# Seven block products for the last 22 gate tiles, and a new start, in a hybrid encoder layer on one core

## What is computed

```python
u = x @ w_in[l]                                # 1024 x 1024 times 1024 x 7688
ua, ub, uc, ug = _split(u, GROUP_COLS)         # gated DeltaNet, RWKV-7, window attention, gates
oa = _gdn_branch(ua, ...)                      # chunks of 64 tokens: inverse of (I + lower) per chunk and head
ob, v_first = _rwkv7_branch(ub, ...)
oc = _swa_branch(uc, swa_sinks[l])
gates = jax.nn.sigmoid(ug).reshape(bsz, t, N_BRANCH, d)        # 3072 columns: 24 tiles of 128
merged = gates[:, :, 0] * (oa @ w_branch_a[l]) + ...
```

## Time and profile before

| What | Value |
|---|---|
| median of three executions | 1816.58 us |
| span of the profiled execution | 1816.2 us (0.4 us under the median) |
| TensorE matmuls busy | 1781.5 us, 98% of the span |
| VectorE, ScalarE, GpSimd busy | 63%, 37%, 32% |
| DMA | 293 MB, 161 GB/s on average |
| stage one | 0 to 749 us, of it the last 22 tiles from about 508 us |
| stage two (scan) | 749.6 to about 922 us |
| stage three | the rest |

### The profile page before, as it was taken

One profiled execution on the slowest core, in us unless ns is written; L12 is line 12 of the kernel. 1 busy time (PEld: TensorE's weight loads), 2 busy tenths in 40 slices (PEclk: granted clock), 3 DMA queues, 4 the chain that ended last, 5 costly groups with the idle time before them and its releaser, 6 DMA issues. The chain is left out here.

```text
span 1816.2 us, 28096 instructions
## 1 busy us (share of the span) xinstructions
PE 1781.5 (98%) x11148; PEld 1471.3 (81%) x11148; DVE 1141.4 (63%) x1354; ACT 665.2 (37%) x1126; POOL 584.6 (32%) x418
## 2 busy tenths in 40 slices
PE   8999999999999999999999999999999999999997
PEld 7778787777788888788878788888888888888886
DVE  2856665666419930377768854966666665665577
ACT  3534434244421211355542231343333333344341
POOL 1211222212213332344415452755455554500000
PEclk9999999999999999999999999999999999999999
DMA  6255575235673377377665573225545455488464
GB/s 178 50 112 140 141 180 138 65 76 155 166 206 93 93 162 228 126 237 245 186 211 173 163 236 97 101 70 183 171 133 171 143 175 179 139 286 300 169 226 155
DMA packets 386434, 293.24 MB, mean 161 GB/s; under 512 B 172428, under 2 KB 318412, under 8 KB 384256
## 3 DMA queue, kind: packets, MB, share of 16 engines
q1 hardware_dynamic: 310080, 237.63, 44.1%
q10 hardware_dynamic: 76224, 53.81, 10.3%
HBM read 196.33 MB, written 94.98 MB: 160 GB/s over the span
## 5 line engine op out<-in xcount | busy, mean ns | idle before, releaser
L168 PE MATMUL bank<-xhi,w_hi 128*128 128x512 f32 x960 | 379.0, 395 | 2.5 <-ACT turned L847 1.7
L170 PE MATMUL bank<-xhi,w_lo 128*128 128x512 f32 x960 | 374.4, 390 | 0.0
L169 PE MATMUL bank<-xlo,w_hi 128*128 128x512 f32 x960 | 373.8, 389 | 0.0
L472 POOL TENSOR_TENSOR w_lo<-w_raw,w_hi 128x1024 fp32r<-128x1024 f32 x59 | 168.3, 2853 | 538.1 <-ACT w_hi L854 538.1
L168 PEld LDWEIGHTS bank<-xhi,w_hi 128*128 128x128 f32 x960 | 180.3, 188 | 43.3 <-issue 6.8
L170 PEld LDWEIGHTS bank<-xhi,w_lo 128*128 128x128 f32 x960 | 180.2, 188 | 38.4
L169 PEld LDWEIGHTS bank<-xlo,w_hi 128*128 128x128 f32 x960 | 180.4, 188 | 36.1
L2044 POOL TENSOR_TENSOR ff_ring_lo<-ff_w_sums,ff_ring_hi 128x512 fp32r<-128x512 f32 x88 | 125.7, 1430 | 74.6 <-ACT ff_ring_hi L2326 74.4
L2044 POOL TENSOR_TENSOR ff_ring_lo<-ff_raw,ff_ring_hi 128x512 fp32r<-128x512 f32 x66 | 96.2, 1460 | 149.4 <-ACT ff_ring_hi L2326 149.4
L834 ACT ACTIVATE work<-bank 128x512 f32<-128x512 f32 x68 | 40.7, 598 | 244.7 <-PE bank L170 228.4
L175 PE MATMUL b_ps<-x1hi,ff_ring_hi 128*128 128x512 f32 x264 | 102.9, 390 | 0.0
(11 more groups left out here) (418 smaller groups left out, 3968.7 us busy)
## 6 DMA issues: line engine op xcount, KB each, us to landing
w_raw<-in_w_in ACTq DMA_DIRECT2D x61, 512.0 KB, 4.3
hid_ops<-y SPq DMA_DIRECT2D x77, 256.0 KB, 2.8
ff_raw<-hid_ops SPq DMA_DIRECT2D x77, 256.0 KB, 3.9
op<-opnd SPq DMA_DIRECT2D x16, 1152.0 KB, 5.5
u<-work ACTq DMA_DIRECT2D x68, 256.0 KB, 4.3
b_gate<-u SPq DMA_DIRECT2D x24, 512.0 KB, 3.6
ff_raw<-in_ffn_gate SPq DMA_DIRECT2D x22, 512.0 KB, 4.5
ff_raw<-in_ffn_up SPq DMA_DIRECT2D x22, 512.0 KB, 5.7
```

What stands on the lines that cost most here:

```text
L168: pe.matmul(out, w_hi, x_hi, start=first, stop=False)
L169: pe.matmul(out, w_hi, x_lo, start=False, stop=False)
L170: return pe.matmul(out, w_lo, x_hi, start=False, stop=last)
L472: pool.tensor_tensor(w_lo[b][:, :, :], w_raw[b][:, :, :], as_f32(w_hi[b][:, :, :]), ALU.subtract).then_inc(w_lo_done, 1)
```

## The change

1. The last 22 gate tiles are taken as 11 pairs. Three blocks of x (512 inner by 512 tokens) and four sums of blocks, made once, are multiplied with blocks and sums of blocks of the pair's weights: seven products of 12 matmuls a pair (`product`), 77 in all, in the order of `seven_products(11)`. ScalarE makes the high part of each product's weights and GpSimd the low part, in a ring of four; VectorE makes four weight sums a pair and adds products to results held in SBUF (`settle`); ScalarE moves first parts out of PSUM (`snap`), applies the sigmoid (`close`) and stores.
2. The inversion is issued in between: in each slot j of VectorE's loop over the 77 products, from slot 12 on, as many of its instructions as fit a written-out room of 2.5 us less 0.7 us for each other instruction. `settle(j)` waits for the end of product j.
3. Ahead of the block's end only chunk 0 is loaded and waited for. Chunk 1 is issued after product (7, 10) without waiting for it; chunk 2 is loaded in the scan, after the first quarter of the attention's operands and the signal for chunk 1.
4. Start: 28 idle matmuls of 128 columns run on TensorE ahead of the first turn; the first weight load is issued after the first tile of x has landed, not at once.
5. The tile of the attention's values is moved forward in the order, with its own buffer, and its two turns come after RWKV's. The last two turns of head 3 follow products 0 and 1.
6. The gpsimd DMA scratch is cut to 512 (no transfer is issued there), and tiles are laid out anew.

```diff
+IDLE_PRODUCTS = 28
...
-    fillers = [*range(U_SQ, U_SV), *range(U_Z, A_TILES), U_SV, *range(U_GATE, U_GATE + 24)]
+    fillers = [U_SQ, U_SV, *range(U_SQ + 1, U_SV), *range(U_Z, A_TILES), *range(U_GATE, U_GATE + 24)]
...
+NR, NPAIRS = 39, 11
...
+    PAIRS = [(ORDER[NR + 2 * f], ORDER[NR + 2 * f + 1]) for f in range(NPAIRS)]
+    ORDER = ORDER[:NR]
...
-        turn_after[max(at + 1, 2 * at_tile[U_SV] + 2) + g] = ("value", g)
+        turn_after[max(q for q in turn_after if turn_after[q][0] == "rwkv") + 1 + g] = ("value", g)
...
+    LATE = [turn_after[q] for q in sorted(turn_after) if q >= NQ]
...
         def _(pool):
+            pool.memset(work[:, 17, 0:P], 0.0).then_inc(early_zeroed, 1)
...
+            def low_part(i):
+                p, f = SEQ[i]
+                src = pair_raw[f % 2][:, raw_block[p], :] if p in raw_block else part_sum[p]
+                pool.wait_ge(w_hi_done, NT_IN + i + 1)
+                pool.tensor_tensor(lo_pair[:, slot_of(i), :], src, as_f32(hi_pair[:, slot_of(i), :]), ALU.subtract).then_inc(w_lo_done, 1)
...
-            for c in range(DEEP):
-                load_chunk(sp, c, early, opnd, xinv, early_landed, early_inv)
-                sp.wait_ge(early_landed, 112 * c + 112)
-                sp.wait_ge(early_inv, 48 * c + 48)
+            load_chunk(sp, 0, early, opnd, xinv, early_landed, early_inv)
+            sp.wait_ge(early_landed, 112)
+            sp.wait_ge(early_inv, 48)
             sp.wait_ge(cols_landed, 16 * 17)
+            sp.wait_ge(mm_p, AT[7, NPAIRS - 1] + 1)
+            load_chunk(sp, 1, early, opnd, xinv, early_landed, early_inv)
...
+            pe.wait_ge(early_zeroed, 1)
+            for _ in range(IDLE_PRODUCTS):
+                pe.matmul(bank[3][:, 0:P], work[:, 17, 0:P], work[:, 17, 0:P], start=True, stop=True)
             pe.wait_ge(const_landed, 16)
...
+            def product(i):
+                p, f = SEQ[i]
+                pe.wait_ge(w_lo_done, NT_IN + i + 1)
...
+                for k in range(4):
+                    cols_ = slice(k * P, (k + 1) * P)
+                    last = more_dot(pe, to, hi_pair[:, slot_of(i), cols_], lo_pair[:, slot_of(i), cols_], hi[:, k, :], lo[:, k, :], p in (1, 2, 7) and k == 0)
+                last.then_inc(mm_p, 1)
+            for i in range(len(SEQ)):
+                product(i)
+                if i < len(LATE):
+                    turn_tokens(LATE[i])
...
+            act.wait_ge(x_landed[0], 16)
             load_w(0)
             split(0)
             load_w(1)
...
+            def high_part(i):
...
+                if i < RING:
+                    act.wait_ge(mm_done, done_at[NQ - 3 if i < 2 else NQ - 1])
+                else:
+                    act.wait_ge(mm_p, i - RING + 1)
...
+            def settle(j):
+                p, f = SEQ[j]
+                to, before, src = {2: (11, 1, z_bank), 5: (22, 5, y_bank(f)), 4: (21, 6, y_bank(f))}[p]
+                dve.wait_ge(mm_p, j + 1)
+                dve.wait_ge(snapped, SNAP_AT[before, f])
+                dve.tensor_tensor(result_of(to, f), result_of(to, f), src, ALU.add).then_inc(added, 1)
...
+                        yield 0.07 + (PARTS[k].stop - PARTS[k].start) * i * i * (0.0019 if done % 2 else 0.00115)
+            inversion, room = invert(), 0.0
+            for j in range(len(SEQ)):
+                p, f = SEQ[j]
+                work_now = 0
+                if p in (2, 5, 4) and j < len(SEQ) - 1:
+                    settle(j)
+                    work_now += 1
...
+                for one, pair in todo_now:
+                    weight_sum(pair, one)
+                    work_now += 1
...
+                if j >= INV_FROM:
+                    room += 2.5 - 0.7 * work_now
+                    while room > 0:
+                        took = next(inversion, None)
+                        if took is None:
+                            break
+                        room -= took
...
             for c in range(NCH):
                 b = c % DEEP
                 if c >= DEEP:
...
+                if c == 1:
+                    sp.wait_ge(loaded[0], 224)
+                    sp.sem_inc(landed[1], 112)
+                    sp.wait_ge(loaded[1], 96)
+                    sp.sem_inc(inv_landed[1], 48)
+                if c == 2:
+                    sp.wait_ge(*last_stored)
                     load_chunk(sp, c, tiles, opnd, xinv, landed[b], inv_landed[b])
```

More of the change, by code:

```diff
@@ L280 @@
 DEEP = 3
+CHUNK_WORDS = N_FLAT + 8 * 2 * C + 2 * 8 * C + 3 * NPAIR * NB
+SECOND_THIRD = 2 * CHUNK_WORDS - N_FLAT
+TILE_WORDS = 8 * T + CHUNK_WORDS + 6 * NPAIR * C + N_FLAT
+NR, NPAIRS = 39, 11
 def scan_tiles(sb):
-    loads = lambda name, shape: [sb(f"{name}{b}", [P] + shape) for b in range(DEEP)]
-    op, ar, sv, wv = loads("op", [N_FLAT]), loads("ar", [8, 2, C]), loads("sv", [8, C]), loads("wv", [8, C])
-    packed, corner = loads("inv_packed", [2, NPAIR, NB]), loads("inv_corner", [NPAIR, NB])
+    shapes = (("op", [N_FLAT]), ("ar", [8, 2, C]), ("sv", [8, C]), ("wv", [8, C]), ("inv_packed", [2, NPAIR, NB]), ("inv_corner", [NPAIR, NB]))
+    load = lambda b, some: {name: sb(f"{name}{b}", [P] + shape) for name, shape in some}
+    second = load(1, shapes)
+    third = load(2, shapes[1:])
+    sb("tiles_gap", [P, 8 * T - SECOND_THIRD])
+    first = load(0, shapes)
     inv, join = ([sb(f"{name}{b}", [P] + shape) for b in range(2)] for name, shape in (("inv", [2, NPAIR, C]), ("join", [NPAIR, C])))
-    return op, ar, sv, wv, packed, corner, inv, join
+    third.update(load(2, shapes[:1]))
+    of = lambda name: [tiles[name] for tiles in (first, second, third)]
+    return of("op"), of("ar"), of("sv"), of("wv"), of("inv_packed"), of("inv_corner"), inv, join
 def load_chunk(sp, c, tiles, opnd, xinv, landed, inv_landed):
@@ new lines, in project_and_prepare @@
+        halves = [slice(h * HALF, (h + 1) * HALF) for h in range(2)]
+        block_of = lambda x, k, h: x[:, 4 * k:4 * k + 4, halves[h]]
+        ops = {1: (block_of(xhi, 0, 0), block_of(xlo, 0, 0)), 2: (block_of(xhi, 1, 0), block_of(xlo, 1, 0)),
+               3: (block_of(xhi, 1, 1), block_of(xlo, 1, 1)), 4: (block_of(xhi, 0, 1), block_of(xlo, 0, 1)),
+               5: (t5h[:, :, :], t5l[:, :, :]), 6: (t6h[:, :, :], t6l[:, :, :]), 7: (t7h[:, :, :], t7l[:, :, :])}
+        of_slabs = lambda first: work[:, first:first + 2, :].rearrange("p r (k n) -> p (r k) n", n=HALF)
@@ L1186, in _, with last_sum @@
+            for _ in inversion:
+                pass
+            def last_sum(eng):
+                dve = eng
+                dve.wait_ge(mm_p, len(SEQ))
+                dve.wait_ge(snapped, SNAP_AT[6, NPAIRS - 1])
+                out = result_of(21, NPAIRS - 1)
+                dve.tensor_tensor(out, out, y_bank(NPAIRS - 1), ALU.add).then_inc(added, 1)
             dve.wait_ge(inv_stored, 16 * 4 * R)
@@ L1192, in _ @@
                     step(dve.memset(tile[rwkv_rows(1 - e), 4 * e:4 * e + 4, 1, :], 0.0))
-    return [(u_stored[b], 16 * stores[b]) for b in range(2)], last_half
+    u_last = [kept_at(c, NPAIRS) for c in kept]
+    return u_last, last_half, last_sum, (added, 3 * NPAIRS), kept_at(21, NPAIRS), (early_landed, early_inv)
 def token_major(u):
@@ L1461, in _ @@
         def _(dve):
+            last_sum(dve)
             for e in range(2):
@@ L2703, in hybrid_layer_kernel @@
                         early = scan_tiles(lambda name, shape: sb(first, name, shape))
+                    with ExitStack() as first:
+                        sums = [sb(first, "t" + name, [P, 4, HALF], F32R) for name in ("6_hi", "6_lo", "7_lo", "7_hi")]
                     work = sb(sx, "work", [P, 18, T])
```

291 lines of the change are left out of this document (241 added, 50 removed).

## The result

The changed kernel took 1848.84 us (median of four executions, 1843.54 to 1852.82), the kernel before, run beside it, 1817.38 us: a ratio of 1.0174, 95% interval 1.0157 to 1.0192. The forecast was 1830, with a range up to 1848: right in sign, 0.8 us outside the range, and the difference more than twice as large as forecast. The profiled execution spans 1849.5 us (its own time 1851.21), 33.3 us more than that of before, and lies 2.4 us over its median.

What follows compares the result with a forecast made beforehand. TensorE, its matmuls busy 98% of the span, was taken as the bound. Its 29.9 us saved are all given back, and 3.4 + 3.0 + 5.3 + 1.4 = 13.1 us added to 1816.2 gave about 1830 us, range 1808 to 1848.

Steps and rivals of the forecast that it cites:

- the forecast's chain: Products to inversion to stores and loads to scan: scan at 753.0 us against 749.6, before the start's shift.
- Part 5: Kernel start: weights landing at 15.6 us delay the first product by 5.3 us; TensorE's low clock adds 1.4.
- Part 1: Pair products: seven for eight save TensorE 29.9 us; sums of x, splits, snaps and sigmoids cost nothing.
- Part 2: Inversion between products: VectorE needs 170.5 us for 61 slots, 28.1 of it waits for GpSimd; inversion ends at 715.6.
- Part 3: Inversion's end to scan: stores, chunk loads and start take 37.4 us; scan 3.4 us later than before.
- Part 4: Front of the scan: chunk 1's late signal makes TensorE wait 3.0 us (0 to 5).
- Rival B: Kernel start: weights land early enough and warm turns save 1.5 us; 1822 us in all, chance 0.15.
- C: Inversion slots: VectorE's waits are absorbed, inversion ends at 707.5, 8.1 us earlier; 1822 us, chance 0.11.
- D: VectorE's waits and SyncE's path to the scan: both much quicker, 22.9 us less; 1807 us, chance 0.18.
- E: Inversion slots: VectorE falls far behind, 1.12 us of wait per low part, 40 us more; 1870 us, chance 0.09.

Runs made afterwards that it cites:

- e5: The changed kernel with GpSimd writing zeros for the low parts of the pairs' weights instead of subtracting; 1824.49 us.
- e3: The changed kernel with each inversion step on one element a block instead of i x i, still in slots 12 to 72; 1832.48 us.
- e8: The changed kernel with GpSimd making the first three weight sums of pair 0 ahead of its first low part; 1841.22 us.
- e12: The changed kernel with only the inversion's order changed: the group of one row lags by eight steps; 1843.06 us.
- e1: The changed kernel with its first weight load issued at once, not behind x's first tile, idle products kept; 1839.53 us.
- e6: The changed kernel with the inversion let in from slot 6 on instead of slot 12, same room formula; 1831.21 us.
- e9: The changed kernel with weights loaded at once, pair 0's sums first, inversion from slot 6 (room 2.4), one group lagging, split stores, chunk 1 on ScalarE's queue; 1816.36 us.

## Why the prediction was wrong in size

Against the forecast's chain (scan 759.7 with the start's shift) the scan came 18.7 us late: 3.3 + 7.7 + 6.9 + 0.8, in the order of the parts below.

1. **Part 5, the start**: the mechanism and the weight load were right (landed at 16.75, forecast 15.6). The clock's cost behind the idle time was sized from one short stretch at 1.4 us; it was 2.1, and the late first product 6.4 instead of 5.3. With the 1.5 us of the dense part, which are within the spread of profiles, +3.3.
2. **Part 1, "the sums cost nothing"**: this step failed. It looked for room on VectorE, found 39.8 idle us, and did not ask what GpSimd does in the same microseconds. VectorE's sums of x and GpSimd's first low parts and weight sums stretched each other (3.2 to 3.4 us for 2.29, 2.9 to 3.3 for 1.3), and TensorE, which had nothing else queued, waited: +7.7, of which e5 removed 5.7. It removed GpSimd's own time for low parts with the collision; which of the two weighs more is open.
3. **Part 2, the waits**: the mechanism was right, a size was off. VectorE's own work was forecast at 142.4 and measured at 140.4 in e5. The waits were mis-sized: 0.46 us per low part, taken from the feed-forward part, against 0.60 here (35.6 us for 28.1). The row was of the right kind of GpSimd instruction, but of a VectorE that is busy 64% of the time; that a full VectorE meets more of them is the likely reason, and not shown. The slots came to 177.4 us for 170.5, +6.9. A low part that blocks VectorE for its whole length, 87 us by the prediction's working, was too high for the reason given there: settles and reductions don't collide.
4. **Part 3, the tail**: right, 38.2 for 37.4 (stores 23.3 for 23, chunk 0 8.7 for 8.2, chunk 1 5.7 for 5.7); +0.8.
5. **Part 4, the front**: TensorE waited 3.19 us ahead of `inverse_first` in chunk 0, for 3.0 forecast. The wait is real, but that its size fits is luck: with the same front it was 1.1, 1.5, 0.6 and 0.3 us in e3, e5, e8 and e12. Nor did it reach the end as such: from the first to the last chunk's start it was 163.2 us for 160.7, but 159.7, 160.9, 160.6 and 160.5 in these four. From the scan's start to the end, nine profiles with this front (the changed kernel's, e1 to e6, e8, e12) took 1066.4 to 1071.1 us, 1068.9 on average, the one profile of before 1066.6. So the 4.5 us of the account are one profile's; what the front costs lies somewhere between nothing and that, and stays open.

Rival B (harmless start) and C (VectorE keeps pace) fell at the first product and at VectorE's 176 us; D (collisions vanish, quick stores) is what e5 had to force, and the stores took 23.3 us, not 9.9; E had the right mechanism at a price twice too high. Parts 1 and 2 failed at one thing: what GpSimd's instructions do to VectorE beside them was priced once, in one stage, and at nothing in the other; how far that is the whole of part 1 is the open point above.

## What to carry over

When work is moved into a stretch, list for every engine pair what they will do in the same microseconds, not each engine's idle time: VectorE instructions with two SBUF operands and GpSimd instructions that read SBUF, where they meet, add up as if on one engine. A saving on TensorE is worth nothing if the chain to the next stage (inversion, stores, loads) ends later than TensorE; shorten or advance that chain first, and look at what shares its DMA engines, for loads issued earlier on another queue delayed the one that was waited for. And a load at the start of a kernel should not wait for another one if its small packets then have to share the engines with large ones (here 11.5 us from issue to landing instead of 6.2).

## Not expected of the hardware

- GpSimd and VectorE slow each other in both directions: a low part from 1.3 to 1.95 us, a weight sum from 0.69 to as much as 1.78. VectorE's instructions of the same size with one operand in PSUM stayed at 0.68, its reductions at 0.67; a copy with one operand in SBUF did not stay (1.11 to 1.68 us).
- Zeroing a tile on GpSimd (0.53 us, no SBUF read) does not slow VectorE measurably: 0.69 us a weight sum.
- Idle products of 128 columns in float32 take two matmul records each, so that 28 of them show as 56 and last 9.3 to 9.5 us.
- A chunk load whose first part was issued 4 us earlier gained little by it: from 733 to 744 us of e9 ScalarE's queue (the other chunk and two stores) had 71% of the DMA time and its own queue 26%. Its last pieces needed 8.6 us to land, where in the changed kernel, with no other chunk beside them, they needed 3.4.
